# Seven block products instead of eight in four more chunks of a projection, a square root's argument without a reciprocal, and counts over 16 positions

## Chip, cores, metric

One core of one Trainium2 chip runs the whole program, in float32. The metric is the device time of one execution in microseconds; lower is better. The engines are TensorE (PE; its weight loads are PEld), VectorE (DVE), ScalarE (ACT) and GpSimd (POOL); SyncE (SP) issues most DMAs. Each has its own queue of instructions, worked off in order, and they wait for one another by semaphores.

## What is computed

Two transformer-like blocks in a row, each a token mixer and a mixture of experts, over 512 tokens of width 1024. The change lies in the mixer of the second block:

```python
h = rms_norm(x, norm1_g[l])
z = h @ w_in[l]                                   # 1024 -> 4608 columns
u_pool, u_lru, u_gate = z[..., :o1], z[..., o1:o2], z[..., o2:o3]        # 512, 1024, 1024
g_a = jax.nn.sigmoid(z[..., o3:o4]); g_b = jax.nn.sigmoid(z[..., o4:])   # 1024, 1024
y_a = pooling_mixer(u_pool, ...) @ proj_a[l]
y_b = rglru_mixer(u_lru, u_gate, ...) @ proj_b[l]
x = x + (g_a * y_a + g_b * y_b) @ w_out[l]
...
# pooling_mixer, for each of 4 groups with window w of 2, 4, 8, 16
cnt = jnp.minimum(pos, float(w))                  # pos = 1, 2, ...
pooled.append((cg - prev) / cnt[None, :, None])   # windowed sum over its count
# rglru_mixer, xc = convolution of u_lru with 4 taps
r = sigmoid(heads(xc, w_r) + b_r); i = sigmoid(heads(xc, w_i) + b_i)
log_a = -RG_C * r * softplus(-lam)
a = jnp.exp(log_a)
mult = jnp.sqrt(-jnp.expm1(2.0 * log_a))
h[t] = a[t] * h[t-1] + mult[t] * (i[t] * xc[t])   # an associative scan in the reference
return h * jax.nn.gelu(gate_in)
```

## The kernel before

The function with the change is `combine_and_project`: it adds the expert outputs of the first block, norms, transposes the tokens into `a_t` (8 tiles of 128 input columns by 512 tokens) and makes the projection. Its weights come in nine chunks of 512 output columns (2 MB each, numbered `IN20` to `IN20 + 8`), streamed by SP into a ring of four slots. A chunk is loaded once PE has freed the one four before it. Chunks 0 to 3 hold, in turns, 128 columns of `u_lru` and 128 of `u_gate` (so two LRU tiles n each, n from 0 to 7), chunk 4 holds `u_pool`, chunks 5 to 8 the merge gates `g_a` and `g_b`.

**Chunks 0 to 4, plain.** `product(n, cols)` multiplies one tile of 128 output columns: 8 accumulating matmuls into one of four PSUM banks `pz`. DVE copies the even products out (`copy_out`, into `s.lru`), ACT the odd ones through GELU (into `s.gate`). After a pair of products, PE makes the two head products of an LRU tile (`gates_of`).

**Chunks 5 to 8, with seven block products** (`gate_block`). The chunk is cut into 2 x 2 blocks by output and input columns, the tokens by input columns and token halves. Instead of eight block products there are seven, on sums of blocks (Winograd's form of Strassen's scheme): p1 and p2 on plain blocks, p5, p6, p3, p7 and p4 on sums. Each of the seven is 8 matmuls over 256 tokens (`part`). POOL makes the four weight sums s1, s2, s4, s3 of a chunk (`gate_sums`, two instructions each) and, once, four token sums t1 to t4; ACT moves p1 out; DVE makes seven additions from PSUM (c11, u2, u4, c12, u3, c22, c21). A bank is taken again once the addition that reads it is done, so PE's p1 waits for c12 of the chunk before, p2 for u3, p5 for c22, p6 for c21, p7 for c11 and p4 for u2.

**An LRU tile n.** DVE copies the tile's head weights into `dense` (4 small copies) and makes the convolution with 4 instructions (the last tells `conv`); PE's `gates_of(n)` waits for both. ACT's `coefficients(n)` waits for it and for the tile before (`xdone`), and makes i and r by sigmoid, tanh(z) into `mu`, and a = exp(-z), then the square root of what DVE hands back. DVE's `lru_tail(n)` waits for the exp, prepares the square root's argument as 2 tanh / (1 + tanh) with a reciprocal, multiplies, scans (`tensor_tensor_scan`), and multiplies by the gate (`xdone`). The core of it:

```python
dve.wait_ge(aa, 2 * n + 2)
st.link(ts(inv_[:], mu[:], 1.0, None, ALU.add))
st.link(dve.reciprocal(inv_[:], inv_[:]))
stt(mu[:], mu[:], 2.0, inv_[:], ALU.mult, ALU.mult).then_inc(mu_r, 1)
st.link(tt(i_[:], i_[:], xc[:, n % 2, :], ALU.mult))
dve.wait_ge(mu_q, n + 1)
```

**Pooling.** POOL forms the windowed sums of each group by doubling, multiplies by the reciprocal of the count (`cnt`, four rows of 512 positions, whose reciprocals DVE takes), and subtracts the input; PE multiplies by the group's matrix (`pooled`).

The order of the work is written out by hand, engine by engine, and nothing schedules it anew.

## Time and profile before

| | |
|---|---|
| median of 3 runs | 1373.76 us (1372.82 to 1374.27) |
| the profiled execution | 1377.37 us, its span 1375.6 us |
| PE busy | 1305.0 us, 95% |
| DVE busy | 629.7 us, 46% |
| ACT busy | 335.7 us, 24% |
| POOL busy | 198.4 us, 14% |
| granted TensorE clock, mean | 0.986 |

The span is the time from the first to the last instruction in the trace; the profiled execution's own time has some 1.8 us around it. A busy share is a mean over stages with different limits, so the rows below are read for the stage of the change, which lies between about 700 and 945 us. [...]

### The profile page before, as it was taken

What the parts mean: (1) busy time and instruction counts of PE and PEld (TensorE: products, weight loads), DVE (VectorE), ACT (ScalarE), POOL (GpSimd) and SP (SyncE); (2) the same over time, 40 slices, a digit from 0 to 9 for tenths busy, and PEclk for the clock granted to TensorE, in tenths of its full rate; (3) what the DMA queues carried; (4) which work ended last, traced back from release to release, by engine and by line L of the source; (5) the groups of instructions that cost most, each with busy time, mean ns of one, the idle gap of its engine ahead of it and who ended that gap; (6) DMA issues with size and microseconds to landing.
All of it is one profiled execution on the core that took longest, in us unless ns stands there. A gap on an engine that the chain in (4) does not pass through costs nothing. (4 is left out here: it accounts for less than half of the span.)

```text
span 1375.6 us, 20330 instructions
## 1 busy us (share of the span) xinstructions
PE 1305.0 (95%) x8226; PEld 693.7 (50%) x8226; DVE 629.7 (46%) x1294; ACT 335.7 (24%) x574; POOL 198.4 (14%) x328
## 2 busy tenths in 40 slices
PE   6999999999999995698999999999999999999997
PEld 3555536865456331233374446888874643433332
DVE  7739645446556331121567994232643532111006
ACT  5422342434012110010346552110001111111113
POOL 4100000001000110010320307904400001010000
PEclk9999999999999998899999999999999999999999
DMA  9811110155647999999932111132036488999994
GB/s 373 358 62 62 62 61 20 46 214 216 237 176 281 360 424 425 424 422 425 376 135 101 71 61 61 62 122 77 8 136 285 153 317 342 421 392 420 391 418 194
DMA packets 43247, 316.06 MB, mean 230 GB/s; under 512 B 7166, under 2 KB 7174, under 8 KB 24208
## 3 DMA queue, kind: packets, MB, share of 16 engines
q1 hardware_dynamic: 35112, 296.34, 54.2%
q0 software_dynamic: 7584, 17.33, 3.3%
q8 instruction: 66, 1.08, 0.3%
q10 hardware_dynamic: 456, 1.08, 0.2%
q14 instruction: 29, 0.24, 0.0%
HBM read 302.11 MB, written 22.56 MB: 236 GB/s over the span
## 5 line engine op out<-in xcount | busy, mean ns | idle before, releaser
L2235 PE MATMUL m_ps<-store,par 128*32 128x512 f32 (+2 forms) x896 | 148.6, 594 | 0.0
L2235 PE MATMUL mix_ps<-store,par 128*32 128x512 f32 (+2 forms) x688 | 119.4, 611 | 24.7 <-DMA store<-in_gu 14.5
L1135 PE MATMUL mix_ps<-y_t,store 128*128 128x512 f32 x320 | 142.7, 599 | 0.0
L2904 PE MATMUL mix_ps<-y_t,store 128*128 128x512 f32 (+1 forms) x384 | 139.2, 521 | 1.4 <-ACT y_t L3038 1.4
L2904 PEld LDWEIGHTS mix_ps<-y_t,store 128*128 128x128 f32 x384 | 72.8, 190 | 66.0 <-issue 62.8
L1135 PEld LDWEIGHTS mix_ps<-y_t,store 128*128 128x128 f32 x320 | 59.2, 190 | 71.6 <-issue 70.7
L2129 POOL DMA_INDIRECT y_t<-x_rows,m_token x25 | 25.5, 1019 | 458.4 <-DVE m_token L2115 201.8
L2377 DVE TENSOR_TENSOR m2r_a<-m2r_a,m_ps 128x256 f32<-128x256 f32 x22 | 9.3, 421 | 171.0 <-ACT m2r_a L2298 171.0
L2235 PEld LDWEIGHTS m_ps<-store,par 128*32 128x32 f32 (+2 forms) x896 | 46.0, 119 | 81.2 <-issue 81.2
L2235 PEld LDWEIGHTS mix_ps<-store,par 128*32 128x32 f32 (+2 forms) x688 | 36.4, 121 | 90.7 <-issue 90.7
L2257 PE MATMUL m_ps<-store,m2r_a 128*32 128x512 f32 (+2 forms) x448 | 76.3, 595 | 0.6 <-ACT m2r_a L2302 0.6
L2257 PE MATMUL mix_ps<-store,m1r_a 128*32 128x512 f32 (+2 forms) x344 | 60.6, 625 | 9.6 <-issue 7.9
L2377 DVE TENSOR_TENSOR m1r_a<-m1r_a,mix_ps 128x256 f32<-128x256 f32 x16 | 6.8, 422 | 113.8 <-ACT m1r_a L2298 113.8
L1785 PE MATMUL m_ps<-store,y_t 128*128 128x512 f32 x128 | 57.2, 597 | 0.0
L2935 PE MATMUL mix_ps<-y_t,store 128*128 128x256 f32 x224 | 49.7, 379 | 0.0
L2235 PE MATMUL mix_ps<-mods,par 128*32 128x512 f32 (+1 forms) x96 | 47.0, 647 | 0.0
L2935 PEld LDWEIGHTS mix_ps<-y_t,store 128*128 128x128 f32 x224 | 42.6, 190 | 7.1 <-issue 1.4
L3378 PE MATMUL m_ps<-store 128*128 128x256 f32 x192 | 42.8, 379 | 2.3 <-PEq L3529 2.3
L2257 PEld LDWEIGHTS m_ps<-store,m2r_a 128*32 128x32 f32 (+2 forms) x448 | 22.6, 119 | 42.8 <-issue 42.8
L1785 PE MATMUL mix_ps<-store,y_t 128*128 128x512 f32 x96 | 43.6, 600 | 0.0
L2298 ACT ACTIVATE m2r_a<-m_ps 128x256 f32<-128x256 f32 x22 | 8.4, 384 | 141.2 <-PE m_ps L2235 141.2
L2235 PE MATMUL m_ps<-mods,par 128*32 128x512 f32 (+1 forms) x160 | 42.3, 593 | 0.0
(807 smaller groups left out, 2142.4 us busy)
## 6 DMA issues: line engine op xcount, KB each, us to landing
store<-in_gu SPq DMA_DIRECT2D x52, 2048.0 KB, 15.4
store<-in_dn SPq DMA_DIRECT2D x52, 1024.0 KB, 15.4
store<-in_w_in SPq DMA_DIRECT2D x14, 2048.0 KB, 11.0
store<-in_w_ada SPq DMA_DIRECT2D x12, 2048.0 KB, 9.1
mods<-in_gu SPq DMA_DIRECT2D x8, 2048.0 KB
store<-in_w_out SPq DMA_DIRECT2D x4, 2048.0 KB, 8.1
mods<-in_dn SPq DMA_DIRECT2D x8, 1024.0 KB
store<-y_rows SPq DMA_DIRECT2D x8, 1024.0 KB, 9.9
```

The costliest lines, as they stand in the source:

```text
L1135: last = pe.matmul(ps[:, bank_of(n), :], w[:, k, j * P:(j + 1) * P], m.a_t[:, k, :], start=(k == 0), stop=(k == KD - 1))
L1785: last = pe.matmul(ps[:, n % 2, :], m.y_t[:, k, t * P:(t + 1) * P], w[:, k, :], start=(k == 0), stop=(k == KD - 1))
L2129: pool.indirect_dma_start(to, None, c.x_rows, bass.IndirectOffsetOnAxis(c.token[:, i:i + 1], 0), bounds_check=T - 1, oob_is_err=False).the ...
L2235: last = pe.matmul(ps[who, 2 + j % 2, :], xt[:, k, who], w[:, k, :], start=(k == 0), stop=(k == KD - 1))
L2257: last = pe.matmul(ps[who, 6 + q, :], ht[:, k, who], w[:, k, q * HALF:(q + 1) * HALF], start=(k == 0 and v == 0), stop=(k == 1 and v == HV ...
L2298: act.activation(hs[:], ps[:, 2 + j % 2, 0:256], ACT.Silu).then_inc(sl, 1)
L2377: dve.tensor_tensor(h[:], hs[:], ps[:, 2 + j % 2, 256:512], ALU.mult).then_inc(hr, 1)
L2904: last = pe.matmul(pz[:, n % 4, cols], w[:, k, j * P:(j + 1) * P], m.a_t[:, k, cols], start=(k == 0), stop=(k == KD - 1))
L2935: last = pe.matmul(pz[:, bank, half_t[p]], left(p)[:, k, :], right[:, k, :], start=(k == 0), stop=(k == 3))
L3378: last = pe.matmul(self.bank(w, bank)[:, p * HALF // 2:(p + 1) * HALF // 2], left[:, k, p * P:(p + 1) * P], right[:, k, :], start=(k == 0) ...
```

## The change

The chunks 1 to 4 are also made with seven block products (`seven(q)` for q from 1 to 8; chunk 0 stays plain). Their weight sums come from POOL (`weight_sums`), their additions go to DVE in place of the copies, the GELUs read SBUF instead of PSUM, and the work on the LRU tiles is laid between the additions: in chunk q PE makes the head products of the tiles 2q-2 and 2q-1, and DVE their tails, while it prepares the tiles 2q and 2q+1. `lru_tail` forms the square root's argument as (1 + a * a) * tanh(z), which is the same number, so the instruction that added 1 and the reciprocal go, and a square is added. The counts are held for the first 16 positions alone, with one reciprocal over 64 numbers, and the rest is multiplied by the constant 1/w. Two buffers of the pooling move from `mods` to the place of the head weights.

PE's queue around the end of chunk 0 (L2904 is `product`, L2896 transposes tokens, L2919 and L2933 are the head products, L2949 the block products; a row counts matmuls). Before, chunk 0 is made in halves of 256 tokens, and from then on head products and pairs of products over 512 tokens take turns, eight times:

```order
L2904 MATMUL mix_ps<-y_t,store 128x256 x24
L2896 MATMUL mix_ps<-ident,store 128x128 x16
L2904 MATMUL mix_ps<-y_t,store 128x256 x40
L2919 MATMUL mix_ps<-mods,t_row 128x512 x2
L2904 MATMUL mix_ps<-y_t,store 128x512 x16
```

And now, behind chunk 0, the whole of chunk 1: p1 and p2 (x16), head products, p5 and p6 (x16), head products, then p3, p7 and p4:

```order
L2949 MATMUL mix_ps<-y_t,store 128x256 x16
L2933 MATMUL mix_ps<-mods,t_row 128x512 x2
L2949 MATMUL mix_ps<-m1r_a,mods 128x256 x16
L2933 MATMUL mix_ps<-mods,t_row 128x512 x2
L2949 MATMUL mix_ps<-y_t,mods 128x256 x8
L2949 MATMUL mix_ps<-y_t,store 128x256 x8
L2949 MATMUL mix_ps<-masks,store 128x256 x8
```

A chunk has 56 matmuls over 256 tokens where it had 32 over 512, and the same four head products.

DVE's queue for one LRU tile before (L3203 the copy out of PSUM, L3253 the head weights, L3257 to L3260 the convolution, L3208 to L3216 the tail of the tile before, L3265 the reciprocals of the counts):

```order
L3203 COPY store<-mix_ps 128x512
L3253 COPY t_row<-store 64x64 x4
L3257 TENSOR_SCALAR mods<-store,par 128x512
L3258 SCALAR_TENSOR_TENSOR mods<-store,par,mods 128x511
L3259 SCALAR_TENSOR_TENSOR mods<-store,par,mods 128x510
L3260 SCALAR_TENSOR_TENSOR mods<-store,par,mods 128x509
L3208 TENSOR_SCALAR mods<-mods 128x512
L3209 RECIPROCAL mods<-mods 128x512
L3210 SCALAR_TENSOR_TENSOR mods<-mods 128x512
L3211 TENSOR_TENSOR mods<-mods 128x512
```

And now, the second half of a chunk (L3250 to L3257 a tail, L3356 the addition c21, L3290 the head weights, L3300, L3301, L3297 and L3298 the convolution, L3331 the addition c11 of the next chunk):

```order
L3250 TENSOR_TENSOR mods<-mods 128x512
L3251 SCALAR_TENSOR_TENSOR mods<-mods 128x512
L3252 TENSOR_TENSOR mods<-mods 128x512
L3254 TENSOR_TENSOR mods<-mods 128x512
L3255 SCALAR_TENSOR_TENSOR store<-mods 128x512
L3257 TENSOR_TENSOR store<-store 128x512
L3356 TENSOR_TENSOR store<-store,mix_ps 128x2x256
L3290 COPY t_row<-store 64x64 x4
L3300 TENSOR_SCALAR mods<-store,par 128x512
L3301 SCALAR_TENSOR_TENSOR mods<-store,par,mods 128x511
L3297 SCALAR_TENSOR_TENSOR mods<-store,par,mods 128x510
L3298 SCALAR_TENSOR_TENSOR mods<-store,par,mods 128x509
```

The reciprocals are gone, c21 and its kin stand among the LRU work, and the convolution of a tile waits for an addition.

POOL's queue after the token sums, where before the sums of one chunk (L3128 to L3136) were followed by the first pooling group (L3155 on):

```order
L3128 TENSOR_TENSOR par<-store 128x512 x2
L3131 TENSOR_TENSOR store<-par,store 128x512 x2
L3134 TENSOR_TENSOR store<-store 128x512 x2
L3136 TENSOR_TENSOR store<-store 128x4x128 x2
L3155 COPY mods<-store 128x512
```

Now the sums of the chunks 2, 3, 4 and 5 stand there one behind the other, before any pooling; the rows of chunks 3 and 4:

```order
L3160 TENSOR_TENSOR mods<-store 128x512 x2
L3163 TENSOR_TENSOR mods<-mods,store 128x512 x2
L3167 TENSOR_TENSOR mods<-store,mods 128x512 x2
L3169 TENSOR_TENSOR store<-store 128x4x128 x2
L3160 TENSOR_TENSOR par<-store 128x512 x2
L3163 TENSOR_TENSOR store<-par,store 128x512 x2
```

The sums of chunk q wait until PE has freed chunk q - 2. The diff, with renumbering of semaphore counts left out:

```diff
-        def gate_block(q):
+        def seven(q):
...
             part(0, w11, b_of[0, 0]).then_inc(mm, 1)
...
             part(1, w12, b_of[1, 0]).then_inc(mm, 1)
+            if q < GATES2:
+                gates_of(2 * q - 2)
+            if q > 1:
                 added_up(pe, q - 1, "c22")
...
             part(2, s1, t_of[1]).then_inc(mm, 1)
...
             part(3, s2, t_of[2]).then_inc(mm, 1)
+            if q < GATES2:
+                gates_of(2 * q - 1)
...
-        for n in range(20):
-            if n % 4 == 0:
-                m.stream.wait(pe, IN20 + n // 4)
-            if n >= 4:
-                copied_out(pe, n - 4)
-            last = product(n, slice(HALF // 2, HALF) if n < 4 else slice(0, HALF))
-            if n % 4 == 3:
-                m.stream.free(last, IN20 + n // 4)
+        for n in range(4):
+            last = product(n, slice(HALF // 2, HALF))
+            if n == 3:
+                m.stream.free(last, IN20)
             else:
                 last.then_inc(mm, 1)
-            if n % 2 and 3 <= n < 19:
-                gates_of((n - 3) // 2)
-        for q in range(4):
-            if q in (1, 2):
-                pooled(2 * q - 2)
-            gate_block(q)
+        for q in range(1, NIN2):
+            if q in (6, 7):
+                pooled(2 * q - 12)
+            seven(q)
...
             act.activation(r[:], r[:], ACT.Exp, scale=c8[:, 0, n:n + 1]).then_inc(aa, 1)
-            act.wait_ge(mu_r, n + 1)
-            act.activation(mu[:], mu[:], ACT.Sqrt).then_inc(mu_q, 1)
...
-        for n in range(8):
-            product_of(act, 2 * n + 1)
-            act.activation(s.gate[:, n, :], pz[:, (2 * n + 1) % 4, :], ACT.Gelu_apprx_tanh).then_inc(ev_a, 1)
-            if n:
-                coefficients(n - 1)
-        coefficients(7)
-        act.wait_ge(xdone, 8)
-        act.wait_ge(dense_r, 32)
+        def coefficients_end(n):
+            act.wait_ge(mu_r, n + 1)
+            act.activation(mu[:], mu[:], ACT.Sqrt).then_inc(mu_q, 1)
+
+        def gelu(q, what, row):
+
+            added_up(act, q, {"top": "c12", "low": "c21"}[what])
+            act.activation(row, row, ACT.Gelu_apprx_tanh).then_inc(ev_a, 1)
...
-        for q in range(4):
-            if q in (1, 2):
-                pooled(2 * q - 2)
-            top, low = rows_at[2 * q], rows_at[2 * q + 1]
+        for n in range(2):
+            product_of(act, 2 * n + 1)
+            act.activation(s.gate[:, n, :], pz[:, 2 * n + 1, :], ACT.Gelu_apprx_tanh).then_inc(ev_a, 1)
+        for q in range(1, NIN2):
+            top, low = rows_at[q]
+            if q in (6, 7):
+                pooled(2 * q - 12)
             multiplied(act, q, "p1")
             act.activation(top[:, :, half_t[1]], both_p(0), ACT.Copy).then_inc(ev_a, 1)
-            if q in (1, 2):
-                pooled(2 * q - 1)
-            added_up(act, q, "c12")
-            act.activation(top, top, ACT.Sigmoid).then_inc(ev_a, 1)
-            added_up(act, q, "c21")
-            act.activation(low, low, ACT.Sigmoid).then_inc(ev_a, 1)
+            if q < GATES2:
+                coefficients(2 * q - 2)
+                coefficients_end(2 * q - 2)
+                coefficients(2 * q - 1)
+                if q < 4:
+                    gelu(q, "top", s.gate[:, 2 * q, :])
+                coefficients_end(2 * q - 1)
+                if q < 4:
+                    gelu(q, "low", s.gate[:, 2 * q + 1, :])
+            else:
+                if q == GATES2:
+                    act.wait_ge(xdone, 8)
+                    act.wait_ge(dense_r, 32)
+                if q in (6, 7):
+                    pooled(2 * q - 11)
+                added_up(act, q, "c12")
+                act.activation(top, top, ACT.Sigmoid).then_inc(ev_a, 1)
+                added_up(act, q, "c21")
+                act.activation(low, low, ACT.Sigmoid).then_inc(ev_a, 1)
...
-        def gate_sums(q):
+        st.link(pool.iota(per_count[:, 3, :], [[1, 16]], base=0, channel_multiplier=0, allow_small_or_imprecise_dtypes=True))
+        for g in range(3):
+            st.link(pool.tensor_scalar(per_count[:, g, :], per_count[:, 3, :], 1.0, float(2 << g), ALU.add, ALU.min))
+        pool.tensor_scalar(per_count[:, 3, :], per_count[:, 3, :], 1.0, 16.0, ALU.add, ALU.min).then_inc(cnt_r, 1)
+
+        def weight_sums(q, begin, end):
...
+            if begin:
+                m.stream.wait(pool, IN20 + q)
+                if q > 2:
+                    m.stream.wait_used(pool, IN20 + q - 2)
+                for p in range(2):
+                    pool.tensor_tensor(s1[p], w21(p), block_of(q, 1, 1, p), ALU.add).then_inc(sums_r, 1)
+                for p in range(2):
+                    weights_added(pool, q, "s1", p)
+                    pool.tensor_tensor(s2[p], s1[p], block_of(q, 0, 0, p), ALU.subtract).then_inc(sums_r, 1)
+            if end:
+                for p in range(2):
+                    weights_added(pool, q, "s2", p)
+                    pool.tensor_tensor(s4[p], block_of(q, 0, 1, p), s2[p], ALU.subtract).then_inc(sums_r, 1)
+                for p in range(2):
+                    pool.tensor_tensor(w21(p), block_of(q, 0, 0, p), w21(p), ALU.subtract).then_inc(sums_r, 1)
...
+        def average(g):
+
+            w = 2 << g
+            added_up(pool, 4, ("c12", "c21")[g // 2])
...
-            st.link(pool.tensor_tensor(src[:], src[:], cnt[:, g, :], ALU.mult))
+            st.link(pool.tensor_tensor(src[:, 0:16], src[:, 0:16], per_count[:, g, :], ALU.mult))
+            st.link(pool.tensor_scalar(src[:, 16:], src[:, 16:], 1.0 / w, None, ALU.mult))
...
-        m.stream.wait_used(pool, GATE0)
-        gate_sums(2)
+
+        pool.wait_ge(ev, 8)
+        pool.tensor_tensor(t_of[1], b_of[0, 1], b_of[0, 0], ALU.subtract).then_inc(token_sums_r, 1)
+        weight_sums(1, True, False)
+        tokens_added(pool, 1)
+        pool.tensor_tensor(t_of[2], b_of[1, 1], t_of[1], ALU.subtract).then_inc(token_sums_r, 1)
+        weight_sums(1, False, True)
+        tokens_added(pool, 2)
+        pool.tensor_tensor(t_of[4], b_of[1, 0], t_of[2], ALU.subtract).then_inc(token_sums_r, 1)
+        m.stream.wait_used(pool, IN20)
+        pool.tensor_tensor(t_of[3], b_of[1, 1], b_of[0, 1], ALU.subtract).then_inc(token_sums_r, 1)
+        pool.wait_ge(fin, NT)
+        for q in range(2, 6):
+            weight_sums(q, True, True)
+        pool.wait_ge(ca, 1)
+        pool.wait_ge(dense_r, 32)
+        average(0)
+        average(1)
+        pool.wait_ge(xdone, 8)
+        weight_sums(6, True, True)
+        average(2)
+        average(3)
+        weight_sums(7, True, True)
         pool.wait_ge(pmm, 2)
-        gate_sums(3)
+        weight_sums(8, True, True)
...
         def lru_tail(n):
 
             dve.wait_ge(aa, 2 * n + 2)
-            st.link(ts(inv_[:], mu[:], 1.0, None, ALU.add))
-            st.link(dve.reciprocal(inv_[:], inv_[:]))
-            stt(mu[:], mu[:], 2.0, inv_[:], ALU.mult, ALU.mult).then_inc(mu_r, 1)
+            st.link(tt(inv_[:], r[:], r[:], ALU.mult))
+            stt(mu[:], inv_[:], 1.0, mu[:], ALU.add, ALU.mult).then_inc(mu_r, 1)
             st.link(tt(i_[:], i_[:], xc[:, n % 2, :], ALU.mult))
             dve.wait_ge(mu_q, n + 1)
             st.link(tt(i_[:], i_[:], mu[:], ALU.mult))
             st.link(dve.tensor_tensor_scan(s.lru[:, n, :], r[:], i_[:], 0.0, ALU.mult, ALU.add))
-            copied_out(dve, 2 * n + 1)
+            gelu_done(dve, n)
             tt(s.lru[:, n, :], s.lru[:, n, :], s.gate[:, n, :], ALU.mult).then_inc(xdone, 1)
 
...
-        for n in range(8):
-            copy_out(2 * n, s.lru[:, n, :])
+        def heads_in(n):
...
-                    dve.tensor_copy(dense[p, b, k, 64 * h:64 * h + 64], s.heads[p, k, n, :]).then_inc(dense_r, 1)
-            o, q = xc[:, b, :], s.lru[:, n, :]
+                    dve.tensor_copy(dense[p, n % 2, k, 64 * h:64 * h + 64], s.heads[p, k, n, :]).then_inc(dense_r, 1)
+
+        def taps_of(n, late):
+
+            o, q = xc[:, n % 2, :], s.lru[:, n, :]
             w = lambda k: taps[:, 4 * n + k:4 * n + k + 1]
+            if late:
+                st.link(stt(o[:, 2:], q[:, :T - 2], w(1), o[:, 2:], ALU.mult, ALU.add))
+                stt(o[:, 3:], q[:, :T - 3], w(0), o[:, 3:], ALU.mult, ALU.add).then_inc(conv, 1)
+                st.link(ts(o, q, w(3), at(m.par, "conv_b2")[:, n:n + 1], ALU.mult, ALU.add))
+                st.link(stt(o[:, 1:], q[:, :T - 1], w(2), o[:, 1:], ALU.mult, ALU.add))
+
+        dve.wait_ge(cnt_r, 1)
+        dve.wait_ge(fin, NT)
+        dve.wait_ge(zeroed, 1)
+        dve.wait_ge(m.heads_in, 32)
+        for n in range(2):
+            copy_out(2 * n, s.lru[:, n, :])
+            heads_in(n)
-            st.link(ts(o, q, w(3), at(m.par, "conv_b2")[:, n:n + 1], ALU.mult, ALU.add))
-            st.link(stt(o[:, 1:], q[:, :T - 1], w(2), o[:, 1:], ALU.mult, ALU.add))
-            st.link(stt(o[:, 2:], q[:, :T - 2], w(1), o[:, 2:], ALU.mult, ALU.add))
-            stt(o[:, 3:], q[:, :T - 3], w(0), o[:, 3:], ALU.mult, ALU.add).then_inc(conv, 1)
-            if n:
-                lru_tail(n - 1)
-            if 2 <= n < 6:
-                dve.wait_ge(cnt_r, n - 1)
-                dve.reciprocal(cnt[:, n - 2, :], cnt[:, n - 2, :]).then_inc(ca, 1)
-        copy_out(16, s.pool[:, 0, :])
-        copy_out(17, s.pool[:, 1, :])
-        lru_tail(7)
-        copy_out(18, s.pool[:, 2, :])
-        copy_out(19, s.pool[:, 3, :])
+            taps_of(n, False)
+            taps_of(n, True)
...
+            if q < GATES2:
+                lru_tail(2 * q - 2)
             multiplied(dve, q, "p3")
             added_up(dve, q, "u4")
             tt(c12, c12, both_p(0), ALU.add).then_inc(ev_v, 1)
+            if q < 4:
+                heads_in(2 * q)
+                added_up(dve, q, "c12")
+                taps_of(2 * q, False)
             multiplied(dve, q, "p7")
             tt(c21, c21, both_p(1), ALU.add).then_inc(ev_v, 1)
             added_up(dve, q, "u3")
             tt(c22, c21, both_p(2), ALU.add).then_inc(ev_v, 1)
+            if q < 4:
+                taps_of(2 * q, True)
+            if q < GATES2:
+                lru_tail(2 * q - 1)
             multiplied(dve, q, "p4")
             added_up(dve, q, "c22")
             tt(c21, c21, both_p(3), ALU.add).then_inc(ev_v, 1)
+            if q < 4:
+                heads_in(2 * q + 1)
+                added_up(dve, q, "c21")
+                taps_of(2 * q + 1, False)
+                taps_of(2 * q + 1, True)
```

## Rows read from the trace of the kernel before

**Rows 1.** The page: span, and the granted clock in 40 slices.
```profile
span 1375.6 us, 20330 instructions
...
PEclk9999999999999998899999999999999999999999
```

**Rows 2.** Windows: busy us of PE, PEld, DVE, ACT, POOL; granted clock; DMA.
```profile
560.00:600.00 40.00, 28.73 (x138) 10.30 (x140) 5.76 (x16) 2.73 (x6) 4.04 (x4) 0.87 1.01 424
...
781.00:808.00 27.00, 27.00 (x65) 11.93 (x64) 25.96 (x34) 18.14 (x20) 0.00 (x0) 1.00 0.22 78
```

**Rows 3.** Timeline of PE (start, us, engine, line): from the end of chunk 0.
```profile
719.57 1.88 PE L2919 MATMUL mix_ps<-mods,t_row 128*128 128x512 f32 x4
721.28 9.18 PE L2904 MATMUL mix_ps<-y_t,store 128*128 128x512 f32 x21
...
843.16 7.07 PE L2935 MATMUL mix_ps<-y_t,store 128*128 128x256 f32 x32
...
867.34 1.02 PE L2929 MATMUL mix_ps<-store 128*128 128x512 f32 x2
868.20 7.07 PE L2935 MATMUL mix_ps<-y_t,store 128*128 128x256 f32 x32
```

**Rows 4.** Groups by line, 715 to 845 us: busy us, mean ns.
```profile
L3209 DVE RECIPROCAL mods<-mods 128x512 f32<-128x512 f32 x8 | 26.8, 3353 | 0.3
...
L3265 DVE RECIPROCAL mods<-mods 128x512 f32<-128x512 f32 x4 | 13.4, 3343 | 0.0
```

**Rows 5.** Timeline of DVE, POOL idle: end of a tail, head weights, convolution.
```profile
745.06 0.69 DVE L3210 SCALAR_TENSOR_TENSOR mods<-mods 128x512 f32<-128x512 f32 x1
...
746.52 0.69 DVE L3213 TENSOR_TENSOR mods<-mods 128x512 f32<-128x512 f32 x1 [0.17 <-ACT mods L3058]
...
749.11 3.34 DVE L3265 RECIPROCAL mods<-mods 128x512 f32<-128x512 f32 x1
...
752.92 0.84 DVE L3253 COPY t_row<-store 64x64 f32<-64x64 f32 x4
...
756.66 0.43 DVE L3208 TENSOR_SCALAR mods<-mods 128x512 f32<-128x512 f32 x1
```

**Rows 6.** Timeline of DVE: the same tail for the next tile.
```profile
760.51 1.56 DVE L3210 SCALAR_TENSOR_TENSOR mods<-mods 128x512 f32<-128x512 f32 x1
761.99 1.75 DVE L3211 TENSOR_TENSOR mods<-mods 128x512 f32<-128x512 f32 x1
...
765.44 2.17 DVE L3214 TENSOR_TENSOR_SCAN store<-mods 128x512 f32<-128x512 f32 x1
...
769.15 3.34 DVE L3265 RECIPROCAL mods<-mods 128x512 f32<-128x512 f32 x1
```

**Rows 7.** Timeline of POOL: a token sum, and weight sums in two places.
```profile
703.66 2.37 POOL L3139 TENSOR_TENSOR m1r_a<-y_t 128x1024 f32<-128x1024 f32 x1 [23.00 <-ACT y_t L3038]
...
761.48 3.38 POOL L3131 TENSOR_TENSOR store<-par,store 128x512 f32<-128x512 f32 x2
764.82 3.85 POOL L3134 TENSOR_TENSOR store<-store 128x512 f32<-128x512 f32 x2
...
872.40 2.52 POOL L3128 TENSOR_TENSOR par<-store 128x512 f32<-128x512 f32 x2
```

**Rows 8.** Timeline, POOL and DVE at the same moment in chunk 5.
```profile
856.84 1.04 POOL L3160 TENSOR_TENSOR mods<-mods 128x511 f32<-128x511 f32 x1
...
857.18 0.69 DVE L3289 TENSOR_TENSOR store<-store,mix_ps 128x512 f32<-128x512 f32 x1 [6.15 <-PE mix_ps L2935]
```

**Rows 9.** Timeline of ACT: a GELU, then the coefficients up to the next table load.
```profile
766.12 0.60 ACT L3086 ACTIVATE store<-mix_ps 128x512 f32<-128x512 f32 x1 [2.08 <-PE mix_ps L2904]
769.30 1.28 ACT L3052 ACT_TABLE_LOAD   x1 [2.59 <-DVE store L3216]
...
774.66 1.28 ACT L3058 ACT_TABLE_LOAD   x1
```

**Rows 10.** DMA issues between 699 and 702 us: KB each, us to landing.
```profile
store<-in_w_in SPq DMA_DIRECT2D x2, 2048.0 KB, 10.6
```

More of the change, by code:

```diff
@@ L2797, in combine_and_project @@
     xc = m.mods[:, 0:2 * T].rearrange("p (b t) -> p b t", b=2)
-    r, i_, mu, inv_, w2, w3 = (part(n) for n in range(2, 8))
-    cnt = m.mods[:, 8 * T:12 * T].rearrange("p (g t) -> p g t", g=4)
+    r, i_, mu, inv_ = (part(n) for n in range(2, 6))
+    w2, w3 = (m.big[:, 12288 + n * T:12288 + (n + 1) * T] for n in range(2))
     mm, ev_a, ev_v = sem("mm"), sem("eva"), sem("evv")
@@ L2826, in multiplied @@
         if what == "p4":
-            m.stream.wait_used(eng, GATE0 + q)
+            m.stream.wait_used(eng, IN20 + q)
         else:
-            eng.wait_ge(mm, MM0 + 6 * q + ("p1", "p2", "p5", "p6", "p3", "p7").index(what) + 1)
+            eng.wait_ge(mm, MM0 + 6 * (q - 1) + ("p1", "p2", "p5", "p6", "p3", "p7").index(what) + 1)
     def added_up(eng, q, what):
-        eng.wait_ge(ev_v, EV_V0 + 7 * q + ("c11", "u2", "u4", "c12", "u3", "c22", "c21").index(what) + 1)
+        eng.wait_ge(ev_v, EV_V0 + 7 * (q - 1) + ("c11", "u2", "u4", "c12", "u3", "c22", "c21").index(what) + 1)
     def moved_out(eng, q, what):
-        eng.wait_ge(ev_a, EV_A0 + 3 * q + ("p1", "top", "low").index(what) + 1)
+        eng.wait_ge(ev_a, EV_A0[q] + ("p1", "top", "low").index(what) + 1)
     def weights_added(eng, q, what, p):
-        eng.wait_ge(sums_r, SUMS0 + 8 * q + 2 * ("s1", "s2", "s4", "s3").index(what) + p + 1)
+        eng.wait_ge(sums_r, SUMS0 + 8 * (q - 1) + 2 * ("s1", "s2", "s4", "s3").index(what) + p + 1)
     def tokens_added(eng, n):
@@ L2976, in gate_block @@
             added_up(pe, q, "u2")
-            m.stream.free(part(3, w22, t_of[4]), GATE0 + q)
+            m.stream.free(part(3, w22, t_of[4]), IN20 + q)
         last_rows(pe, c, x, last_in)
@@ L3277, in merge_sums @@
             st.link(tt(t[4], b[1, 0], t[2], ALU.subtract))
-        for q in range(4):
-            if q == 3:
+        for q in range(1, NIN2):
+            if q == NIN2 - 1:
                 dve.wait_ge(pev, 4)
@@ L3283, in vector @@
                 merge_sums("b")
-            (c11, c12), (c21, c22) = ([rows[:, :, h] for h in half_t] for rows in rows_at[2 * q:2 * q + 2])
+            (c11, c12), (c21, c22) = ([rows[:, :, h] for h in half_t] for rows in rows_at[q])
             moved_out(dve, q, "p1")
```

102 lines of the change are left out of this document (40 added, 62 removed).

## The prediction

> **What bounds the kernel now.** I began with the page: the span and the slices of the granted clock [rows 1]. The clock is full wherever PE works without a break, so what counts is how much work PE has and where it waits. Then the windows over the stage of the change: in 27 us PE is busy for 27.00, while DVE is busy for 25.96 and ACT for 18.14 [rows 2]. Two engines are nearly full there, and the faster of them decides nothing as long as it stays faster: PE sets the end, and DVE is right behind it.
>
> The timeline of PE gives the length of the stage. The first head products start at 719.57, the block products of chunk 5 at 843.16 [rows 3]: 123.6 us for 16 plain products and 8 pairs of head products. A pair takes 721.28 - 719.57 = 1.71 us, eight of them 13.7, which leaves 109.9 us for the products, 6.87 us each and 27.5 us a chunk. A chunk of seven block products, with one pooling matmul left out, runs from 843.16 to 867.34, that is 24.18 us. PE has no gap in either.
>
> **What PE saves.** Four chunks go from 27.5 to 24.18 us. The stage becomes 4 x 24.18 + 13.7 = 110.4 us instead of 123.6: **13.2 us less**, if PE never waits. With its head products a new chunk takes 24.18 + 3.42 = 27.6 us instead of 30.9. That is the term that is certain.
>
> **What DVE saves and gets.** It loses 8 reciprocals of 512 columns (26.8 us) and 4 of the counts (13.4 us) [rows 4], and ten copies out of PSUM. It gets 28 additions from PSUM, at 0.69 us each [rows 8] 19.3 us, and eight squares, 5.5 us at the same price. The sum goes down, so DVE as a total is not the bound. What could bind is the order: DVE now serves PE's banks and the LRU tiles in one queue, and POOL works at the same time.
>
> **What POOL does to DVE.** Two stretches of DVE's timeline show the same five instructions, from the one that tells the square root to the multiplication by the gate. With POOL idle they take 749.11 - 745.06 = 4.05 us [rows 5]; one tile later 769.15 - 760.51 = 8.64 us [rows 6]. In between lie no waits that explain it: the instructions themselves grew, from 0.69 to 1.56 and 1.75 us, the scan to 2.17. POOL made weight sums at that time, and these grew as well: a pair takes 2.52 us elsewhere and 3.38 and 3.85 there [rows 7]. So an instruction of DVE that reads two operands in SBUF pays about 0.95 us beside a stream of POOL's additions. An addition that reads one operand from PSUM does not: 0.69 us in the middle of a POOL addition [rows 8]. Before, this happened once in the stage, for one tile's tail; now POOL adds weights in each of the chunks 1 to 4, about 10 us alone (four pairs at 2.5) and some 14 us when contended, and in the chunks 2 to 4 it may start as soon as PE has freed the chunk before, so at the very beginning, where DVE makes the odd tile's tail.
>
> **The loop that closes.** I follow DVE from the addition u2 of one chunk to that of the next, by the order written in the change:
> - u2 and u4: 2 x 0.69 = 1.4 us.
> - The even tile's tail: the square 0.65, then the five instructions above with the square root between them, 4.05: 4.7 us.
> - ACT's coefficients of the odd tile, which wait for that tail: from 769.30 to 774.66 [rows 9], 5.4 us. DVE makes c12, u3, c22 and the next tile's convolution meanwhile, all hidden.
> - The odd tile's tail. ACT has a GELU in front of the square root, each with a table load: 2 x (1.28 + 0.6) = 3.8 us, then multiplication, scan and multiplication, 749.11 - 746.52 = 2.6: 6.4 us with POOL idle. Contended, DVE is the later: 8.64 for the five and 1.6 for the square: 10.3 us.
> - c21: 0.7 us. Then head weights and convolution of the next odd tile: 756.66 - 752.92 = 3.7 us [rows 5], and up to 2.1 more (two times 0.95 and a little) if POOL is still at it; six of POOL's eight instructions are used up by the tail.
> - c11: 0.7 us.
>
> The sum is 1.4 + 4.7 + 5.4 + 6.4 + 0.7 + 3.7 + 0.7 = **23.0 us** with POOL out of the way, and **26.9 to 29.0** with it, plus some five handovers between engines at about 0.1 to 0.17 us (the 0.17 in [rows 5]), 0.6 us: 27.5 to 29.6. PE's chunk takes 27.6. So the loop either just fits or exceeds PE's time by up to 2.0 us. PE would meet it at the second pair of head products of the chunks 2, 3 and 4, where it waits for the convolution that stands last in DVE's queue; behind it queue p3, p7 and p4. I take 1.5 us in each of three chunks, nearer to the upper end, since the four small copies of the head weights also move data within SBUF: **4.5 us lost**, with 0 and 6.0 as bounds.
>
> The Trainium skill, SBUF — State Buffer, "SBUF: two separate sides", says why the rows look so: VectorE and GpSimd share a pair of ports which is "an exclusive lock, not a bandwidth split", held for a whole instruction. The trace agrees: a DVE instruction grew by about one of POOL's, not by a factor (0.69 by 0.9 to 1.06 us, the scan by 0.95). By that rule the small copies would be blocked one by one, and the loop would come out at its upper end, 29.6 us, with 6.0 us lost and the time at 1367.6; if instead the two engines shared evenly by the ratio 4.05 to 8.64, the loop would be nearer 28.4 and the loss 2.4 us.
>
> **Smaller terms.** The tail of tile 7 now meets the pooling averages of POOL in chunk 5, which start when c12 of chunk 4 is done. Its six instructions may grow by 0.95 each, 5.7 us, and c21 of chunk 4 must come before p6 of chunk 5, which starts 3 x 3.45 = 10.4 us into it; uncontended it comes some 5.7 us in, so contended at about 11.4: I take 1.0 us, bounds 0 and 1.4. The start: POOL makes t1 from 703.66, 2.4 us [rows 7]; the weights of chunk 1 are issued at about 701 and land 10.6 us later at the latest [rows 10], so at 711.6. Eight sums at 1.25 to 1.9 and three token sums at 2.4 end at 711.6 + 22.4 = 734 at the latest, while p5 of chunk 1, which needs only four of them and t1, starts at 719.57 + 6.9 + 1.7 = 728.2 and p7 at 740.4. Nothing waits: nothing is added. The later weight sums of chunks 5 to 8 have their old distance to PE: hidden by 10 us of block products or more. The counts over 16 positions shorten POOL by some us at a place where it is idle otherwise, and free DVE of four reciprocals already counted. GELU from SBUF costs ACT the same 0.6 us; ACT's total of 18 in 27 us leaves it room. Everything behind chunk 8 is released by PE's own progress and moves forward as a whole.
>
> **The sum.** 13.2 - 4.5 - 1.0 = 7.7 us. The profiled execution took 1377.37 us, 3.6 more than the median of the runs, with the same stage in it; its sum would be 1369.7, and against the median 1373.76 - 7.7 = **1366.0 us**.
>
> **The rivals.**
> - *PE never waits* (chance 0.14). For it: the lower end of the loop, 27.5, is PE's own time, and DVE's instructions could fall into POOL's gaps. Against it: the five together took 8.64 us, and hardly one found a gap [rows 6]. It gives 13.2 less, 1360.6 us.
> - *The loop takes most of the gain* (0.12). If the head weights and all of the convolution are blocked too, every one of POOL's eight instructions blocks DVE: the loop is 23.0 + 0.6 + 8 x 0.95 = 31.2 us, 3.6 us are lost in each of three chunks, 11.8 with the small term: 1372.4 us, and with a part of it hidden anything from 1369 on. Half of this case lies within 0.2% of no change.
> - *Slower* (0.08). The place is the odd tile's tail with the head weights behind it, and the price is what a blocked instruction waits. The step from 0.95 to 1.9 us, which is the mean length of POOL's own slowed additions (3.85 for two) [rows 7], makes eight of them cost 15 us; the loop is then 23.0 + 0.6 + 15 less the 2 us that hide under ACT, 36.8 us, and PE waits 9.2 us in each of three chunks: 27.6 - 12.2 = 15.4 slower, 1389 us. It decides from a loop of 27.6 + 12.2 / 3 = 31.7 us on. Against it speaks that the five lost 4.59 us together, 0.92 each [rows 5, 6].
>
> A lower clock is not counted beside these: in the window where PE was idle for 28% of the time it was granted 0.87 [rows 2], while a wait of 1.5 us in 29 is 5%.
>
> **Numbers.** The main case, a loop of 28.2 to 29.9 us, has 0.66 and gives 1363 to 1369; the others follow as above. What a measurement of this kernel tells from no change is about 0.2%, 2.7 us. Faster than 1371.0: 0.66 + 0.14 + half of 0.12 = 0.86; within 0.2%: 0.06; slower: 0.08. The range runs from the case without waits to the edge of the main case and a part of the next, 1360.3 to 1371.0.
>
> **What would show it.** In the trace after: a chunk's seven parts still at 3.45 us each and 110 us plus waits between the first head products and chunk 5; waits of 1 to 2 us in front of the second head products of the chunks 2, 3 and 4, put down to DVE's last convolution instruction; tail instructions of odd tiles at 1.6 us and of even ones at 0.69; no wait for weight sums. Wrong would be: waits in front of p5, p6 or p1, which would mean that an addition is late and the loop is longer than I count; or tails that are not slowed. The forecast falls if the loop is above 31 us, or if ACT and not DVE is last in it.

## The result, and the profile of the changed kernel

The changed kernel takes **1366.18 us** (median of 4 runs, 1364.69 to 1367.16), the kernel before 1373.86 (4 runs, 1372.82 to 1374.27). The ratio is 0.9941 [0.9930, 0.9952]: 7.7 us less, as the sum of the forecast had it. The profiled run took 1365.87 us. One execution of the kernel before beside the last four experiments took 4583 us; it is left out of their ratios. First the page of the changed kernel: span, busy time by engine, granted clock in 40 slices.

```profile
span 1364.1 us, 20798 instructions
...
PE 1293.8 (95%) x8418; PEld 731.1 (54%) x8418; DVE 638.4 (47%) x1301; ACT 338.0 (25%) x578; POOL 243.7 (18%) x364
...
PEclk9999999999999997899999999999999999999999
```

The window that answers to the second of [rows 2] (busy us of PE, PEld, DVE, ACT, POOL; granted clock; DMA):

```profile
781.00:808.00 27.00, 25.66 (x115) 21.54 (x114) 25.99 (x36) 18.69 (x21) 11.01 (x8) 1.00 0.22 76
```

In the stage of the change PE is no longer busy without a break: 25.66 of 27 us. DVE is busy for 25.99 us, as before, although the reciprocals are gone: POOL is now busy beside it for 11.01 us, and was not at all. What that does to DVE's instructions, its timeline shows further down. The clock stayed full, so the idle time cost nothing beyond itself.

Now PE's timeline from the second changed chunk on (start, us, engine, line; in brackets the idle time in front and who ended it). It answers to [rows 3]. A float32 matmul leaves two records in a trace, so the eight matmuls of a block product are x16. The chunks begin at 714.05, 741.95, 771.75, 800.94, and chunk 5 at 829.56.

```profile
741.95 7.07 PE L2949 MATMUL mix_ps<-y_t,store 128*128 128x256 f32 x32
...
755.38 3.72 PE L2949 MATMUL mix_ps<-m1r_a,store 128*128 128x256 f32 x16 [1.18 <-DVE store L3356]
759.60 1.95 PE L2933 MATMUL mix_ps<-mods,t_row 128*128 128x512 f32 x4 [0.51 <-issue]
...
771.75 7.07 PE L2949 MATMUL mix_ps<-y_t,store 128*128 128x256 f32 x32
...
780.38 7.07 PE L2949 MATMUL mix_ps<-m1r_a,mods 128*128 128x256 f32 x32
788.79 1.96 PE L2933 MATMUL mix_ps<-mods,t_row 128*128 128x512 f32 x4 [1.34 <-issue]
...
817.40 1.96 PE L2933 MATMUL mix_ps<-mods,t_row 128*128 128x512 f32 x4 [0.77 <-issue]
...
829.56 7.07 PE L2949 MATMUL mix_ps<-y_t,store 128*128 128x256 f32 x32
...
853.73 1.02 PE L2943 MATMUL mix_ps<-store 128*128 128x512 f32 x2
```

The four chunks take 27.90, 29.80, 29.19 and 28.62 us, together 829.56 - 714.05 = 115.51, where it was 123.6: **8.1 us less**. A chunk that never waits would take 27.6, as forecast; what is above it (0.3, 2.2, 1.6, 1.0, together 5.1) is waiting, in front of the second head products in the chunks 3 and 4, and in chunk 2 in two places, the larger one in front of p6. The row says "issue" for the head products, so the profile names nobody. The row of DVE that ends just before suggests who was late: the convolution's last instruction, at 787.94 + 0.75 = 788.69, and PE goes on at 788.79. Chunk 5 takes 853.73 - 829.56 = 24.17 us, without a wait, as before.

DVE's timeline around the third changed chunk: an even tile's tail, then the odd tile's, with copies of head weights. It answers to [rows 5, 6].

```profile
760.01 0.68 DVE L3333 TENSOR_TENSOR store<-store,mix_ps 128x512 f32<-128x512 f32 x1
...
761.87 0.69 DVE L3250 TENSOR_TENSOR mods<-mods 128x512 f32<-128x512 f32 x1 [0.38 <-ACT mods L3068]
...
764.78 1.22 DVE L3255 TENSOR_TENSOR_SCAN store<-mods 128x512 f32<-128x512 f32 x1
...
766.65 0.68 DVE L3341 TENSOR_TENSOR store<-store,mix_ps 128x512 f32<-128x512 f32 x1
...
772.26 1.78 DVE L3250 TENSOR_TENSOR mods<-mods 128x512 f32<-128x512 f32 x1
...
779.12 2.17 DVE L3255 TENSOR_TENSOR_SCAN store<-mods 128x512 f32<-128x512 f32 x1
...
782.83 0.67 DVE L3356 TENSOR_TENSOR store<-store,mix_ps 128x512 f32<-128x512 f32 x1
783.42 2.33 DVE L3290 COPY t_row<-store 64x64 f32<-64x64 f32 x4
...
787.94 0.75 DVE L3298 SCALAR_TENSOR_TENSOR mods<-store,par,mods 128x509 f32<-128x509 f32 x1
...
789.20 0.68 DVE L3333 TENSOR_TENSOR store<-store,mix_ps 128x512 f32<-128x512 f32 x1
```

And POOL's, which adds the next chunk's weights exactly then; it answers to [rows 7]:

```profile
772.06 3.13 POOL L3160 TENSOR_TENSOR par<-store 128x512 f32<-128x512 f32 x2 [16.21 <-PE mix_ps L2949]
775.16 3.38 POOL L3163 TENSOR_TENSOR store<-par,store 128x512 f32<-128x512 f32 x2
778.50 3.86 POOL L3167 TENSOR_TENSOR store<-store 128x512 f32<-128x512 f32 x2
782.31 2.94 POOL L3169 TENSOR_TENSOR store<-store 128x512 f32<-128x512 f32 x2
```

POOL starts 0.31 us after PE has begun the chunk (771.75), so its 13.2 us of additions fall on the odd tail and the copies of DVE. The loop from u2 to u2 is 789.20 - 760.01 = 29.19 us, exactly PE's chunk.

### The profile page after: what moved, and what is told of

Read it like the earlier page. It is cut to its first block and busy times, and to the rows that moved or that the text cites. A ratio compares the mean times of both kernels' runs of the same rounds, so it can differ in the third digit from the quotient of the medians.

```text
span 1364.1 us, 20798 instructions
## 1 busy us (share of the span) xinstructions
PE 1293.8 (95%) x8418; PEld 731.1 (54%) x8418; DVE 638.4 (47%) x1301; ACT 338.0 (25%) x578; POOL 243.7 (18%) x364
## 5 line engine op out<-in xcount | busy, mean ns | idle before, releaser
L1135 PEld LDWEIGHTS mix_ps<-y_t,store 128*128 128x128 f32 x320 | 59.2, 190 | 71.6 <-issue 70.7
L2949 PE MATMUL mix_ps<-y_t,store 128*128 128x256 f32 x432 | 95.8, 379 | 0.0
L2949 PEld LDWEIGHTS mix_ps<-y_t,store 128*128 128x128 f32 x432 | 82.1, 190 | 12.9 <-issue 1.9
L2202 POOL DMA_INDIRECT y_rows<-y_t,m_dest x23 | 23.2, 1007 | 117.4 <-DVE y_t L2386 67.3
L2235 PE MATMUL mix_ps<-mods,par 128*32 128x512 f32 (+1 forms) x96 | 43.7, 609 | 0.0
## 6 DMA issues: line engine op xcount, KB each, us to landing
store<-in_w_in SPq DMA_DIRECT2D x14, 2048.0 KB, 10.6
store<-y_rows SPq DMA_DIRECT2D x8, 1024.0 KB, 10.3
```

The lines of the kernel that those rows point to most:

```text
L1135: last = pe.matmul(ps[:, bank_of(n), :], w[:, k, j * P:(j + 1) * P], m.a_t[:, k, :], start=(k == 0), stop=(k == KD - 1))
L2202: pool.indirect_dma_start(c.y_rows, bass.IndirectOffsetOnAxis(c.dest[:, i:i + 1], 0), out_at(i), None, bounds_check=2 * T - 1, oob_is_err= ...
L2235: last = pe.matmul(ps[who, 2 + j % 2, :], xt[:, k, who], w[:, k, :], start=(k == 0), stop=(k == KD - 1))
L2949: last = pe.matmul(pz[:, bank, half_t[p]], left(p)[:, k, :], right[:, k, :], start=(k == 0), stop=(k == 3))
```

## The experiments

All ran beside the kernel before: the first four on one chip (median of before 1375.23), the last four on another (1375.91). The totals in the expectations go by 1373.8 for the kernel before, so 1.5 to 2.1 us must be added to compare them. A loop here is the round of work of DVE and ACT that has to close once per chunk, from the addition u2 to the next chunk's u2. The theory: PE's 13.2 us are saved in full, and what is lost is the loop of DVE and ACT, made long by POOL's weight sums beside the odd tail. Rivals: the shorter tail and the counts matter by themselves; ACT (a GELU in front of the root) is what makes the loop long; the loop is long whoever runs beside it.

### The square root's argument and the counts alone (e1)

The kernel before with the two small edits, all chunks up to 4 with plain products:

```diff
-            st.link(ts(inv_[:], mu[:], 1.0, None, ALU.add))
-            st.link(dve.reciprocal(inv_[:], inv_[:]))
-            stt(mu[:], mu[:], 2.0, inv_[:], ALU.mult, ALU.mult).then_inc(mu_r, 1)
+            st.link(tt(inv_[:], r[:], r[:], ALU.mult))
+            stt(mu[:], inv_[:], 1.0, mu[:], ALU.add, ALU.mult).then_inc(mu_r, 1)
...
-            st.link(pool.tensor_tensor(src[:], src[:], cnt[:, g, :], ALU.mult))
+            st.link(pool.tensor_tensor(src[:, 0:16], src[:, 0:16], per_count[:, g, :], ALU.mult))
+            st.link(pool.tensor_scalar(src[:, 16:], src[:, 16:], 1.0 / (2 << g), None, ALU.mult))
```

> The kernel before with two of the three parts of the change, the square root's argument without a reciprocal and the counts over 16 positions; the chunks stay plain. My theory (PE sets the stage, DVE is behind it): DVE loses 40 us between 715 and 845 us, PE's stage from the first head products to chunk 5 stays at 123.6 us, and the time is that of before within 0.2% (0 to 1 us less). Rival (the gain of the change comes from taking DVE's load away): most of the 7.7 us appears here already.

Measured: 1374.39 us (11 runs), ratio 0.9992 [0.9983, 1.0001]. PE's timeline, the first head products and chunk 5:

```profile
716.97 1.88 PE L2919 MATMUL mix_ps<-mods,t_row 128*128 128x512 f32 x4
...
840.57 7.07 PE L2935 MATMUL mix_ps<-y_t,store 128*128 128x256 f32 x32
```

The stage takes 123.60 us, as before to a hundredth. The 40 us of reciprocals less on DVE [rows 4] change nothing while PE is the bound.

### The reciprocal back in the changed kernel (e2)

```diff
-            st.link(tt(inv_[:], r[:], r[:], ALU.mult))
-            stt(mu[:], inv_[:], 1.0, mu[:], ALU.add, ALU.mult).then_inc(mu_r, 1)
+            st.link(ts(inv_[:], mu[:], 1.0, None, ALU.add))
+            st.link(dve.reciprocal(inv_[:], inv_[:]))
+            stt(mu[:], mu[:], 2.0, inv_[:], ALU.mult, ALU.mult).then_inc(mu_r, 1)
```

> The changed kernel with the old argument of the square root, so with one instruction more and a reciprocal in each of eight tails. My theory (a loop through DVE and ACT closes at 29 us a chunk and is what PE waits for): the loop gets 2 x 3.1 us longer per chunk, less what POOL gains meanwhile; chunks of 33 to 35.6 us in place of 29, PE's waits 20 to 24 us in place of 4.6, and 1380 to 1388 us, slower than the kernel before. Rival (PE waits for something else, and the tails have slack): within 3 us of the changed kernel.

Measured: 1382.75 us (2 runs), ratio 1.0049 [1.0031, 1.0067], **slower than the kernel before**. The chunks take 28.24, 33.12, 31.55 and 33.75 us, and chunk 5 28.78: 20.9 us above the time without waits, as expected, though one chunk is shorter than the expected 33 to 35.6. PE's and DVE's timelines in the third changed chunk:

```profile
791.38 3.72 PE L2949 MATMUL mix_ps<-m1r_a,mods 128*128 128x256 f32 x16 [3.42 <-DVE store L3357]
```
```profile
782.24 3.35 DVE L3251 RECIPROCAL mods<-mods 128x512 f32<-128x512 f32 x1
...
790.64 0.68 DVE L3357 TENSOR_TENSOR store<-store,mix_ps 128x512 f32<-128x512 f32 x1
```

PE waits in front of p6 for c21, which stands behind the tail. So the edit that is worth nothing alone (e1) is worth 16 us together with the block products (1382.75 and 1366.91 of the repetition below, by their ratios 1.0049 - 0.9933 of 1374): the tail and the block products can't be judged one by one.

### The weight sums of the chunks 3 to 5 left out (e3)

```diff
+            if 3 <= q < 6:
+                one = lambda ap: ap[:, 0:1, 0:4]
+                w21 = lambda p: one(full(q, 1, 0, p))
+                s1, s2, s4 = ([one(ap) for ap in s] for s in s_at[q])
+                b = lambda *at: one(full(*at))
```

> The changed kernel; POOL's weight sums of chunks 3, 4 and 5 are made over 4 of 512 columns only, so the products of these chunks work on stale sums. My theory (DVE's instructions with two operands in SBUF are blocked by POOL's additions): tails of odd tiles at 0.69 us an instruction, no wait of PE in chunks 2 to 4, chunks of 27.6 us, 4.6 us less than the changed kernel: about 1361.6 us. Rival (the waits come from the length of the chain through ACT alone): chunks stay at 29 us and the time at 1366.

Measured: 1498.9 us. That total says nothing about the stage: the chunks now work on stale sums, the numbers behind them are others, and what lies behind the stage takes 670 us instead of 535. That the tokens take other ways through the experts there is my guess, not shown. The stage stands ahead of all that: 28.23, 27.60, 27.61 and 27.61 us a chunk, 111.05 in all. PE's and DVE's timelines where POOL now makes nothing to speak of:

```profile
786.95 1.88 PE L2933 MATMUL mix_ps<-mods,t_row 128*128 128x512 f32 x4
```
```profile
775.21 0.69 DVE L3262 TENSOR_TENSOR mods<-mods 128x512 f32<-128x512 f32 x1 [1.84 <-ACT mods L3097]
775.93 1.22 DVE L3263 TENSOR_TENSOR_SCAN store<-mods 128x512 f32<-128x512 f32 x1
...
778.40 0.85 DVE L3298 COPY t_row<-store 64x64 f32<-64x64 f32 x4
```

No wait is left in the chunks 2 to 4, the tail is at its free length, and now it is DVE that waits for ACT's root (1.84). The loop is short enough when POOL is nearly idle: the third rival falls. My expectation for the whole time was missed, for a reason that has nothing to do with the question.

### The upper GELU behind the root (e4)

```diff
-                if q < 4:
-                    gelu(q, "top", s.gate[:, 2 * q, :])
                 coefficients_end(2 * q - 1)
                 if q < 4:
+                    gelu(q, "top", s.gate[:, 2 * q, :])
                     gelu(q, "low", s.gate[:, 2 * q + 1, :])
```

> The changed kernel with ACT's GELU of the even tile behind the square root of the odd tile instead of in front of it, so that the root may come 1.9 us earlier. My theory (with POOL at work the root waits for DVE's blocked instructions, not for ACT): no change, 1366 us and PE's waits 4 to 4.6 us. Rival (ACT's queue is the long link of the loop): the loop gets 1.9 us shorter and PE's waits vanish, 1361.6 us.

Measured: 1367.79 us (4 runs), ratio 0.9944 [0.9925, 0.9963]; chunks of 28.19, 29.77, 29.20 and 28.64, 115.80 in all. Nothing moved. ACT's timeline in the third changed chunk, first in the changed kernel, then in this run, tells why:

```profile
773.47 0.63 ACT L3102 ACTIVATE store<-store 128x512 f32<-128x512 f32 x1
...
775.78 0.63 ACT L3097 ACTIVATE mods<-mods 128x512 f32<-128x512 f32 x1 [0.38 <-DVE mods L3251]
```
```profile
776.65 0.63 ACT L3097 ACTIVATE mods<-mods 128x512 f32<-128x512 f32 x1 [2.31 <-DVE mods L3250]
```

The root waits for DVE in both. In the changed kernel the GELU and the table load behind it are done 0.38 us before DVE hands over the argument; without them in front ACT waits 2.31 us, and the root comes 4.03 us into the chunk as it did. The margin is small, but there is a second one: DVE comes to the instruction that needs the root only at 777.45, 1.04 us after the root is done (776.41).

### The weight sums in two parts, away from the tails (e5)

POOL's sums of the chunks 3 to 5 are no longer released by PE alone: s1 and s2 wait for c11 of the chunk before, s4 and s3 for its c22. Behind c11 DVE adds from PSUM or waits for PE, behind c22 it still waits for ACT's coefficients of the odd tile, so a part of each half was to fall into time that DVE has to spare.

```diff
+                if 3 <= q < 6:
+                    added_up(pool, q - 1, "c11")
                 for p in range(2):
                     pool.tensor_tensor(s1[p], w21(p), block_of(q, 1, 1, p), ALU.add).then_inc(sums_r, 1)
...
             if end:
+                if 3 <= q < 6:
+                    added_up(pool, q - 1, "c22")
```

> The changed kernel; POOL's weight sums s1 and s2 of the chunks 3 to 5 wait for DVE's addition c11 of the chunk before, s4 and s3 for its c22, so that they no longer stand beside the odd tile's tail but beside additions from PSUM and DVE's waits. My theory: no work is taken away, only the overlap, and the tail of the odd tile is free again: chunks 2 to 4 at 27.6 to 28 us, PE's waits under 1 us, about 4.5 us less than the changed kernel, 1361.7 us (0.9910 of before). Rival (the sums cost the same wherever they lie, since DVE has no slack): the chunks stay at 29 us and the time at 1366.

Measured: 1364.35 us (5 runs), ratio 0.9910 [0.9893, 0.9927]. Chunks of 28.53, 27.61, 27.60 and 27.61 us, 111.35 in all, 4.2 less than the changed kernel. The ratio is the expected one. PE's, POOL's and DVE's timelines in the third changed chunk:

```profile
788.93 1.88 PE L2933 MATMUL mix_ps<-mods,t_row 128*128 128x512 f32 x4
```
```profile
772.59 3.38 POOL L3171 TENSOR_TENSOR mods<-store,mods 128x512 f32<-128x512 f32 x2 [8.96 <-DVE store L3353]
...
787.65 2.54 POOL L3162 TENSOR_TENSOR par<-store 128x512 f32<-128x512 f32 x2 [8.32 <-DVE store L3335]
```
```profile
774.77 1.76 DVE L3254 TENSOR_TENSOR mods<-mods 128x512 f32<-128x512 f32 x1
...
779.91 0.69 DVE L3258 TENSOR_TENSOR mods<-mods 128x512 f32<-128x512 f32 x1
```

POOL does the same work and DVE too. Not all of the overlap is gone: four of the eight additions still slow the convolution's last instruction and the first three of the odd tail (1.76; ACT's root waits 1.22 us for it), and the other four reach into the start of the next even tail. But the odd tail's second half, the copies and the convolution behind them are free, and PE has no wait in the chunks 2 to 4. That is enough.

### The weight sums late, in one part (e6)

The same with the first wait only, so that all eight additions follow c11 at a stretch:

```diff
+                if 3 <= q < 6:
+                    added_up(pool, q - 1, "c11")
```

> As the one before, but all four sums of a chunk begin at c11 of the chunk before, in one piece. My theory: the first half is free, the second meets the even tile's tail: chunks of 27.6, 28.8 and 29.6 us, PE's waits about 3 us, 1364.3 us. Rival (only the odd tile's tail matters): like the two parts, 1361.7 us.

Measured: 1367.31 us (4 runs), ratio 0.9941 [0.9925, 0.9957]. Chunks of 28.09, 27.61, 28.55 and 29.03; chunk 5 takes 26.35, where it is 24.17. PE's timeline:

```profile
799.68 7.14 PE L2949 MATMUL mix_ps<-y_t,store 128*128 128x256 f32 x32 [0.78 <-DVE store L3343]
...
841.14 3.72 PE L2949 MATMUL mix_ps<-m1r_a,mods 128*128 128x256 f32 x16 [1.83 <-DVE store L3358]
```

Now the even tail is slowed and c12 behind it is late; PE waits for it in front of p1, 0.78 us here and 0.98 a chunk later. The lost time has not gone, it has moved: above the time without waits lie 2.4 us in the chunks 2 to 4, where the changed kernel has 4.8, and 2.2 more in chunk 5, which I had not expected. Against the two parts (e5) the total is 3.0 us higher, where 2.6 was expected. It isn't enough to move POOL's work off the odd tail in one piece; in two pieces, a part of it in time that DVE spends on PSUM or waiting, it cost nothing (e5).

### Both together, and the changed kernel again (e7, a2)

e7 has the edits of e4 and e5.

> The sums in two parts and ACT's GELU of the even tile behind the square root of the odd tile. With POOL out of the way the loop through ACT is the longer one, about 23 us, still under PE's 27.6: no further gain over the sums in two parts alone. Rival (some wait is left and it comes from ACT's queue): up to 1 us less than the two parts alone.

Measured: 1365.02 us (4 runs), ratio 0.9918 [0.9902, 0.9934], the stage 110.73 us. The total is not to be told from e5. The stage is 0.6 us shorter, all of it in chunk 1 (27.91 us against 28.53), which lies between these bounds in every version with block products; the chunks 2 to 4 have no wait in either, so ACT's order has nothing left to give there.

> The changed kernel itself, beside the others on the same chip: 0.994 of before, PE's waits 4.6 us in chunks 1 to 4.

Measured: 1366.91 us (5 runs), ratio 0.9933 [0.9919, 0.9947]; chunks of 28.05, 29.77, 29.17 and 28.62, with the same waits (1.16, 0.50, 1.33, 0.77). So the stage, 115.61 us, repeats to 0.1 us in a second execution. All nine runs of e5 and e7 (1359.99 to 1365.70) lie below all five of this one (1365.73 to 1367.89), by 2.1 us in the medians: e5 is the fastest version measured, though its own interval overlaps that of the changed kernel. The medians (1364.35 and 1366.91) lie only 2.6 us apart, where the stage gained 4.2. PE's start into the stage and a dip of the clock behind it, both described below, differ by 2 to 3 us from execution to execution; whether they make up the rest is not shown.

## Why the prediction was right

**What PE saves: right.** Chunks without waits take 27.60 us (e3, e5), and 4 x 27.6 is the forecast 110.4.

**The loop: right, at its upper end.** By the terms of the forecast, in the third changed chunk: u2 and u4 1.48 (forecast 1.4), even tail with a handover 5.16 (4.7), ACT's coefficients 5.61 (5.4), odd tail 772.26 to 782.83 = 10.57 (10.3), c21 0.59 (0.7), head weights and convolution 5.19 (3.7 to 5.8), c11 0.59 (0.7). The sum is 29.19, the forecast span 27.5 to 29.6. DVE's round is 29.84 us into chunk 2 (730.17 to 760.01), above the forecast's span, and 28.62 into chunk 4. The waits are 5.1 us over the four chunks, where I had taken 4.5. e3 shows that it is POOL that makes the difference, and e4 that it isn't ACT.

**The lock.** The copies of the head weights tell the two readings of the forecast apart: four of them take 0.84 us free and 1.32, 2.33 and 3.34 in the chunks 2, 3 and 4, so they grow by 0.5, 1.5 and 2.5, in steps of about 1.0, the amount by which one DVE instruction grew in the tails. An even sharing by the forecast's ratio, 8.64 / 4.05 = 2.13, would make of 0.84 at most 1.8. The Trainium skill, SBUF — State Buffer, "SBUF: two separate sides", states a lock that one instruction holds to its end while the other engine is fully blocked; the steps agree with that. By that reading the loop was to be 29.6; it was 29.19 and, in chunk 4, 28.62, since POOL was done before DVE came to the convolution (0.75 us, as when free).

**Where it was off.** The forecast's loss, 4.5 + 1.0 = 5.5 us, was 5.1, but partly by luck: against the forecast the tail of tile 7 cost 1.0 less and chunk 4 0.5 less, chunk 1 cost 0.3, chunk 2 0.7 and chunk 3 0.1 more.
- "Smaller terms", the tail of tile 7: I took 1.0 us, and it was 0. POOL's averages did slow it, but by less. DVE's and POOL's timelines in chunk 5:

```profile
833.68 1.23 DVE L3255 TENSOR_TENSOR_SCAN store<-mods 128x512 f32<-128x512 f32 x1
...
836.21 0.67 DVE L3356 TENSOR_TENSOR store<-store,mix_ps 128x512 f32<-128x512 f32 x1
```
```profile
831.12 0.53 POOL L3179 COPY store<-store 128x1 f32<-128x1 f32 x1
831.73 1.37 POOL L3180 TENSOR_TENSOR store<-store 128x511 f32<-128x511 f32 x1
```

  The tail takes 836.21 - 829.52 = 6.7 us instead of 4.7 free and 10.6 in the third changed chunk, for what the trace shows because every second instruction of the averages is a short one and DVE gets past. c21 is done 7.3 us into the chunk, and PE wants it after 10.4.
- Chunk 2's larger wait stands in front of p6, which I had called a sign that the loop is longer than I count. There it was: the odd tail began 2.17 us into chunk 2 (744.12), and 0.51 us into chunk 3 (772.26). DVE's timeline, the even tail of chunk 1 and the convolution in front of the odd one:

```profile
732.60 1.65 DVE L3251 SCALAR_TENSOR_TENSOR mods<-mods 128x512 f32<-128x512 f32 x1
...
742.56 1.64 DVE L3298 SCALAR_TENSOR_TENSOR mods<-store,par,mods 128x509 f32<-128x509 f32 x1
```

  POOL's sums of the start-up ran until 733.71 and slowed that even tail by 1.3 us, and its next sums, begun at 742.26, slowed the convolution by 0.9. Before that, the copies and the convolution of tile 1 took from 716.61 to 729.65, 13.0 us beside POOL instead of 3.7; PE waited for them, and chunk 1 lost 0.3. This is the term that I had booked as "nothing is added": I had compared POOL's end, 734 at the latest, with what PE needs, and not with what DVE does meanwhile. That this start-up is the reason I read from the trace; no run takes it away alone. Without POOL beside chunk 2's odd tail it does no harm (e3, e5: 27.6).
- Against the medians the total fell by 7.7 us, in the profile the stage by 8.1. Between the two profiled executions lie 11.5 us: 5.5 ahead of the stage (714.05 and 719.57), 8.1 in it, and 2.1 given back behind it, 1.7 of these by the dip of the clock described at the end. The way to the stage differs without the change too: chunk 1 begins at 717.22 in the repetition of the changed kernel, so some 3 us lie between executions of one kernel, and e1 reaches the stage at 716.97. What makes these differences stays open.

**The rivals.** That PE never waits is what the chunks 2 to 4 of e5 and e3 show, but only with POOL moved or nearly idle. That the loop takes most of the gain, or more, needed a loop above 31 us; with the reciprocal the chunks 2 to 4 take 31.55 to 33.75, and that kernel is indeed slower (e2).

## What to carry to other kernels

Before shortening the engine that is the bound, follow the loop of the engines that serve it through one period, with the durations that they have when the others run beside them; here 4 us of head room (27.6 against 23.0 + 0.6 by the forecast's sum with POOL idle) became 1.6 us of waits. In these traces a DVE instruction with both operands in SBUF pays about 1 us beside a stream of GpSimd's 512-wide additions (0.69 to 1.64 or 1.78), one with an operand in PSUM nothing (0.67 to 0.69). So put GpSimd's work where DVE reads PSUM or waits, in pieces, and not simply "as early as the buffer is free". An edit that is worth nothing while another engine is the bound (e1) can decide whether the next one gains or loses (e2).
